# The end of a hybrid S5 and retention block: the first half's norm beside the last product, the last block taken from PSUM, rows of x loaded ahead, the last rows in halves

## The reference

```python
def reference(x, ...):                      # x: 1024 rows of 2048, float32
    h = rms_norm(x, norm_pre)
    proj = h @ w_in
    u_s, z_s, q, k, v, z_r, gl_s, gl_r = jnp.split(proj, SPLIT_IDX, axis=-1)
    y_s = s5_mixer(u_s, ...) * jax.nn.silu(z_s)
    y_r = retention(q, k, v) * jax.nn.silu(z_r)
    m = sigmoid(gl_s) * (y_s @ w_proj_s5) + sigmoid(gl_r) * (y_r @ w_proj_ret)
    return x + rms_norm(m @ w_out, norm_post)

def rms_norm(x, gain):
    return x * rsqrt(mean(x * x, axis=-1) + EPS) * gain
```

## Time and profile before

| What | Value |
|---|---|
| median of 3 runs | 2310.22 us (2309.75 to 2310.89) |
| profiled execution, time | 2312.22 us |
| profiled execution, span from first to last instruction | 2310.4 us |
| TensorE, share of the span | 96% |
| VectorE | 79% |
| ScalarE | 51% |
| mean rate of the DMA engines | 210 GB/s |
| mean granted TensorE clock | 0.99 |

### The profile page before, as it was taken

One profiled execution on the slowest core, in us unless ns is written; L12 is line 12 of the kernel. 1 busy time (PEld: TensorE's weight loads), 2 busy tenths in 40 slices (PEclk: granted clock), 3 DMA queues, 4 the chain that ended last, 5 costly groups with the idle time before them and its releaser, 6 DMA issues.

```text
span 2310.4 us, 28465 instructions
## 1 busy us (share of the span) xinstructions
PE 2212.9 (96%) x10212; PEld 1817.7 (79%) x10212; DVE 1814.9 (79%) x2937; ACT 1177.3 (51%) x1974; POOL 122.4 (5%) x200
## 2 busy tenths in 40 slices
PE   6989999999999999999989999999999999999993
PEld 3778788788888888888867878888888788788883
DVE  4986996888898888655897867766788889977676
ACT  4334444556665455564434645755545554445552
POOL 5240000000000000000000000200000000000000
PEclk9999999999999999999999999999999999999997
DMA  7347558776577365579755789575846755644546
GB/s 259 146 164 219 155 169 270 251 256 216 179 263 241 106 234 169 200 261 325 235 174 155 257 264 281 170 239 191 304 142 202 238 178 187 247 166 130 161 134 268
DMA packets 265854, 485.58 MB, mean 210 GB/s; under 512 B 51648, under 2 KB 59856, under 8 KB 263536
## 3 DMA queue, kind: packets, MB, share of 16 engines
q1 hardware_dynamic: 218336, 398.54, 52.4%
q10 hardware_dynamic: 37712, 50.47, 6.3%
q0 software_dynamic: 9664, 34.75, 4.7%
HBM read 367.28 MB, written 116.39 MB: 209 GB/s over the span
## 4 chain that ended last, share of the span: by engine, by line
PE 75%; DVE 14%; DMA 5%; issue 3%; ACT 2%; ACTq 0%; SPq 0%; DVEq 0%
PE psum L1803 18%; PE psum L1805 18%; PE psum L1804 18%; PE psum L1799 6%; PE psum L1801 6%; PE psum L1800 5%; DMA araw<-aops 4%; DVE a_lo L1291 3%; DVE b_lo L1293 3%; DVE work L1545 1%; ACT a_hi L886 1%; DVE keep L1301 1%; DVE work L1257 1%; PE psum L1740 1%; PE psum L1822 1%
## 5 line engine op out<-in xcount | busy, mean ns | idle before, releaser
L1803 PE MATMUL psum<-a_hi,b_hi 128*128 128x512 f32 x2352 | 923.5, 393 | 32.5 <-DVE b_lo L1293 32.1
L1805 PE MATMUL psum<-a_lo,b_hi 128*128 128x512 f32 x2352 | 918.1, 390 | 0.0
L1804 PE MATMUL psum<-a_hi,b_lo 128*128 128x512 f32 x2352 | 917.5, 390 | 0.0
L886 ACT ACTIVATE a_hi<-araw 128x512 fp32r<-128x512 f32 x644 | 406.0, 630 | 875.8 <-PE psum L1805 642.8
L1291 DVE TENSOR_TENSOR a_lo<-araw,a_hi 128x512 fp32r<-128x512 f32 x644 | 444.8, 691 | 348.4 <-ACT a_hi L886 345.3
L1803 PEld LDWEIGHTS psum<-a_hi,b_hi 128*128 128x128 f32 x2352 | 443.0, 188 | 138.1 <-DVE b_lo L1293 40.1
L1805 PEld LDWEIGHTS psum<-a_lo,b_hi 128*128 128x128 f32 x2352 | 442.9, 188 | 93.2
L1804 PEld LDWEIGHTS psum<-a_hi,b_lo 128*128 128x128 f32 x2352 | 443.4, 188 | 91.7 <-issue 0.7
L1293 DVE TENSOR_TENSOR b_lo<-bx,b_hi 128x512 fp32r<-128x512 f32 x432 | 296.8, 687 | 0.0
L895 ACT ACTIVATE b_hi<-bx 128x512 fp32r<-128x512 f32 x432 | 266.4, 617 | 1.6 <-DMA bx<-in_wstream 1.5
L1799 PE MATMUL psum<-b_hi,a_hi 128*128 128x512 f32 x672 | 263.1, 392 | 3.8 <-DVE b_lo L1293 3.4
(11 more groups left out here) (161 smaller groups left out, 1609.5 us busy)
## 6 DMA issues: line engine op xcount, KB each, us to landing
araw<-aops SPq DMA_DIRECT2D x632, 256.0 KB, 3.0
bz<-in_wstream SPq DMA_DIRECT2D x216, 256.0 KB, 4.5
aops<-work SPq DMA_DIRECT2D x28, 1024.0 KB, 6.8
spill<-keep ACTq DMA_DIRECT2D x28, 1024.0 KB, 6.1
bx<-in_wstream SPq DMA_DIRECT2D x108, 256.0 KB, 4.4
by<-in_wstream SPq DMA_DIRECT2D x108, 256.0 KB, 5.3
work<-spill SPq DMA_DIRECT2D x20, 1024.0 KB, 7.3
aops<-work POOLq DMA_DIRECT2D x15, 1024.0 KB, 7.1
```

The source lines that it names most:

```text
L886: A.activation(a_hi[:, r, :], left(s), ACT.Copy).then_inc(head, 1)
L1803: T.matmul(bank, b_hi[:, r, cols], a_hi[:, r, :], start=first, stop=False, skip_group_check=on)
L1804: T.matmul(bank, b_lo[:, r, cols], a_hi[:, r, :], start=False, stop=False, skip_group_check=on)
L1805: done = T.matmul(bank, b_hi[:, r, cols], a_lo[:, r, :], start=False, stop=last, skip_group_check=on)
```

## The change

- SP loads rows 2 to 7 of x during GO1, at steps 44, 46, 48, 50, 53 and 55: rows 2 and 3 into `by`, rows 4 and 5 into `bz`, rows 6 and 7 into `keep` blocks 3 and 2. The loads behind the last split are gone.
- VectorE makes the weights' differences for p = 6 of GO1 during p = 5, behind the splits of the same step, and no longer three steps ahead.
- ScalarE squares the block of p = 5 in two pairs, at steps 51 and 52, in place of four pieces at 52.
- The sum and root of the first half come at step 53, the reciprocal and row 0 at 54, row 1 at 55; rows 2 and 3 follow behind the last splits.
- The block of p = 6 is not evacuated: ScalarE squares its four pieces in PSUM, and VectorE multiplies each by the gain from PSUM once its square is done, the sum of squares before the last piece.
- Rows 4 to 7 are finished and stored in halves of 1024 columns, 512 KB each.

```diff
@@ -242,7 +242,10 @@
         o_row = area(0, 16384).rearrange("p (i n) -> p i n", i=8)
         gain_row = area(16384, 2048)
         x_ring = area(18432, 4096).rearrange("p (s n) -> p s n", s=2)
-        x_late = [by[:, 0:4, :], by[:, 4:8, :], bz[:, 0:4, :], bz[:, 4:8, :]]
+
+        x_rest = {n: b.rearrange("p k m -> p (k m)") for n, b in
+                  ((2, by[:, 0:4, :]), (3, by[:, 4:8, :]), (4, bz[:, 0:4, :]), (5, bz[:, 4:8, :]))}
+        x_rest[6], x_rest[7] = keep[:, 3, :], keep[:, 2, :]
 
         sq_ring = keep[:, :, :]
         rstd = araw[:, 0:2, :]
@@ -638,16 +641,31 @@
                     sp.wait_ge(op_stored[S4], 64)
                     for n in range(2):
                         sp.dma_start(x_ring[:, n, :], x[n]).then_inc(rows_loaded[n], 16)
-            sp.wait_ge(split, 2 * STEPS)
+                if g == GO1 and at in (44, 46):
+                    n = at // 2 - 20
+                    sp.wait_ge(split, 2 * (step_of(g, 4, TILES[g] - 1) + 1))
+                    sp.wait_ge(rows_loaded[n % 2], 16)
+                    sp.dma_start(x_rest[n], x[n]).then_inc(rows_loaded[n % 2], 16)
+                if g == GO1 and at in (48, 50):
+                    n = at // 2 - 18
+                    sp.wait_ge(gained, n - 2)
+                    sp.wait_ge(out_squared, 16 if n == 6 else 20)
+                    sp.wait_ge(rows_loaded[n % 2], 32)
+                    sp.dma_start(x_rest[n], x[n]).then_inc(rows_loaded[n % 2], 16)
+                if g == GO1 and at in (53, 55):
+                    n = (at - 45) // 2
+                    sp.wait_ge(split, 2 * (step_of(g, 5, TILES[g] - 1) + 1))
+                    sp.wait_ge(summed, sums_before(g, 6, TILES[g] - 1) + 1)
+                    sp.dma_start(x_rest[n], x[n]).then_inc(late_loaded, 16)
             for n in range(4):
-                sp.dma_start(x_late[n].rearrange("p k m -> p (k m)"), x[4 + n]).then_inc(late_loaded, 16)
-            for n in range(2, 4):
-                sp.wait_ge(rows_ready, n - 1)
-                sp.dma_start(x_ring[:, n % 2, :], x[n]).then_inc(rows_loaded[n % 2], 16)
-            for n in range(8):
                 sp.wait_ge(rows_ready, n + 1)
                 sp.dma_start(out[n], o_row[:, n, :]).then_inc(out_stored, 16)
-            sp.wait_ge(out_stored, 8 * 16)
+            for n in range(4, 8):
+                for half in range(2):
+                    sp.wait_ge(rows_ready, 2 * n - 3 + half)
+                    cols = slice(D_MODEL // 2 * half, D_MODEL // 2 * (half + 1))
+                    sp.dma_start(out[n][:, cols], o_row[:, n, cols]).then_inc(out_stored, 16)
+            sp.wait_ge(out_stored, 12 * 16)
 
 
         @block.gpsimd
@@ -980,18 +998,21 @@
                 else:
                     act.dma_start(spilled(g, b), kept_4(b)).then_inc(kept_stored[b], 16)
 
-            def squares(g, p):
+            def squares(g, p, first=0, blocks=4):
 
                 b = KEEP[p]
-                if p == 6:
+                if (g, p) == (GO1, 6):
+                    act.wait_ge(step_done, STEPS)
+                elif p == 6:
                     act.wait_ge(act_evac, 4 * g + 4)
                 else:
                     act.wait_ge(dve_evac, 3 * g + p - 2)
-                for n in range(4):
+                for n in range(first, first + blocks):
                     count = 16 * (g - GO0) + 4 * (p - 3) + n
                     if count:
                         act.wait_ge(out_squared, count)
-                    A.activation(m_junk, kept_4(b)[:, n, :], ACT.Square,
+                    block_n = main_banks(g)[:, n, :] if (g, p) == (GO1, 6) else kept_4(b)[:, n, :]
+                    A.activation(m_junk, block_n, ACT.Square,
                                  accum_out=ssq[:, 4 * HALF_OF[b] + n, 2 * (g - GO0) + COL_OF[b]:2 * (g - GO0) + COL_OF[b] + 1]
                                  ).then_inc(out_squared, 1)
 
@@ -1090,7 +1111,7 @@
                 if s == 2:
                     root(1)
                 over = ended(s - 3)
-                if over and over[1] in (0, 1, 2, 6):
+                if over and over[1] in (0, 1, 2, 6) and over != (GO1, 6):
                     evacuate(*over)
                 if over == (GV, 6):
                     take_m2()
@@ -1101,7 +1122,11 @@
                 if over == (GGR0, 6):
                     retain()
                 over = ended(s - 5)
-                if over and over[1] >= 3:
+                if ended(s - 4) == (GO1, 5) or ended(s - 5) == (GO1, 5):
+                    squares(GO1, 5, 2 * (s - BASE[GO1] - 51), 2)
+                elif ended(s - 1) == (GO1, 6):
+                    squares(GO1, 6)
+                elif over and over[1] >= 3 and over != (GO1, 6):
                     if over[0] in (GO0, GO1):
                         squares(*over)
                     else:
@@ -1119,7 +1144,7 @@
                 if s == BASE[GGS1] + 34:
                     shift(1)
                 for i in range(2):
-                    if s == STEPS + (2, 6)[i]:
+                    if s == (BASE[GO1] + 53, STEPS + 2)[i]:
                         act.wait_ge(out_sum, i + 1)
                         A.activation(rstd_out[:, 4 * i:4 * i + 4], rstd_out[:, 4 * i:4 * i + 4], ACT.Sqrt, scale=1.0 / D_MODEL,
                                      bias=eps_sb[:, 0:1]).then_inc(out_std, 1)
@@ -1555,7 +1580,9 @@
                 b = KEEP[p]
                 i = HALF_OF[b]
                 col = COLS * (2 * (g - GO0) + COL_OF[b])
-                if p == 6:
+                if (g, p) == (GO1, 6):
+                    dve.wait_ge(step_done, STEPS)
+                elif p == 6:
                     dve.wait_ge(act_evac, 4 * g + 4)
                 else:
                     dve.wait_ge(dve_evac, 3 * g + p - 2)
@@ -1563,6 +1590,14 @@
                     dve.wait_ge(gain_row_loaded, 16)
                     for op in (A11, S4, S3, A12, A22):
                         dve.wait_ge(op_stored[op], 64)
+                if (g, p) == (GO1, 6):
+                    for n in range(4):
+                        if n == 3:
+                            sum_rows(1)
+                        dve.wait_ge(out_squared, 28 + n + 1)
+                        V.tensor_tensor(o_row[:, 4 + n, col:col + COLS], main_banks(g)[:, n, :], gain_row[:, col:col + COLS],
+                                        ALU.mult).then_inc(gained, 1)
+                    return
                 V.tensor_tensor(o_row[:, 4 * i:4 * i + 4, col:col + COLS], kept_4(b),
                                 gain_row[:, col:col + COLS].unsqueeze(1).broadcast_to([P, 4, COLS]), ALU.mult).then_inc(gained, 1)
 
@@ -1576,15 +1611,17 @@
 
             def finish_row(n):
                 dve.wait_ge(out_inverse, n // 4 + 1)
-                dve.wait_ge(gained, 7 + n // 4)
-                if n < 4:
-                    dve.wait_ge(rows_loaded[n % 2], 16 * (n // 2 + 1))
-                    rows = x_ring[:, n % 2, :]
-                else:
-                    dve.wait_ge(late_loaded, 4 * 16)
-                    rows = x_late[n - 4].rearrange("p k m -> p (k m)")
-                V.scalar_tensor_tensor(o_row[:, n, :], o_row[:, n, :], rstd_out[:, n:n + 1], rows, ALU.mult, ALU.add
-                                       ).then_inc(rows_ready, 1)
+                dve.wait_ge(gained, 7 if n < 4 else 11)
+                if n in (4, 5):
+                    dve.wait_ge(late_loaded, 2 * 16)
+                else:
+                    dve.wait_ge(rows_loaded[n % 2], 16 * {0: 1, 1: 1, 2: 2, 3: 2, 6: 3, 7: 3}[n])
+                rows = x_ring[:, n, :] if n < 2 else x_rest[n]
+                parts = 1 if n < 4 else 2
+                for part in range(parts):
+                    cols = slice(D_MODEL // parts * part, D_MODEL // parts * (part + 1))
+                    V.scalar_tensor_tensor(o_row[:, n, cols], o_row[:, n, cols], rstd_out[:, n:n + 1], rows[:, cols], ALU.mult, ALU.add
+                                           ).then_inc(rows_ready, 1)
 
             for s in range(STEPS + TAIL):
                 if s < STEPS:
@@ -1596,7 +1633,7 @@
                 scanning = 0 <= c < CHUNKS
                 if scanning:
                     scan_products(c)
-                if s + RING < STEPS and not (TILES[place(s + RING)[0]] == 4 and place(s + RING)[1] == 6):
+                if s + RING < STEPS and not (place(s + RING)[1] == 6 and (TILES[place(s + RING)[0]] == 4 or place(s + RING)[0] == GO1)):
                     weights_summed(s + RING)
                 if s < STEPS and TILES[g] == 4 and p == 4:
                     weights_summed(step_of(g, 6, k))
@@ -1604,6 +1641,8 @@
                     scan_sum(c, 0)
                 if s < STEPS:
                     rests(s)
+                if s < STEPS and g == GO1 and p == 5:
+                    weights_summed(step_of(g, 6, k))
                 if scanning:
                     scan_sum(c, 1)
                 over = ended(s - 3)
@@ -1627,8 +1666,14 @@
                     gate_product(GATE_STEP[s])
```

(28 more changed lines are left out.)

## The result

The changed kernel takes **2291.91 us** in the median of 4 runs (2290.64 to 2293.36), the kernel before, beside it, 2310.01 us; the ratio is 0.9922, with a 95% interval of 0.9906 to 0.9938.

The account below looks back on a forecast made before the run. Tail without TensorE bounds it: VectorE's steps, a late x row, a transfer backlog. VectorE's rebuilt chain ends 2290.8, last store 2294.2, plus 0.45 closing: 2294.7, from the median 2294.5; range 2292.5 to 2298.5, the forecast case's own 2292.8 to 2296.

Parts of the forecast that it names:

- First half's norm: Steps 53 to 54: ScalarE's table load and root, 1.49 us together after the sum, start head 54 1.76 us late.
- What bounds the kernel: 35.1 us tail without TensorE, set by VectorE's ten large steps, a late x row and a transfer backlog.
- Loads ahead: Six x row loads during steps 44 to 55 cost 0 us, at most 0.4 per row; 6.71 us wait and backlog go.
- Differences moved, squares in pairs: Differences moved eight steps forward cost 0; third block's squares in two pairs start head 53 at 2261.95.
- Rows 0 and 1: VectorE at steps 54 and 55: row 0 ends 2270.5, splits of 55 at 2271.75, leaving TensorE 0.6 us spare.
- Last block in PSUM: 1.88 us evacuation goes; squares end 2278.4, products and reciprocal 2281.15, PSUM priced as SBUF, up to 0.4 more.
- Halves: Last rows as eight 1024-column steps, 1.20 us apart: 9.6 us against 9.04 for four full rows, VectorE ending 2290.8.
- Stores: No backlog left at the first half; the last 512 KB store lands in 3.2 us plus 0.2, at 2294.2.
- head 54 later: Rival, 0.18: load or a handover costs 1.0 to 2.5 us more, delaying VectorE's chain; 2295.5 to 2297.0 us.
- The stores set the end: Rival, 0.12: the last half store still takes 8.0 us to land; 2299.3, by the median 2299 us.
- The work eats the gain: Rival, 0.06: row steps before the splits make TensorE miss 2.72 us steps; two missed give 2299.9, four 2305.4.
- Slower: Rival, 0.02: x loads hold back araw, TensorE loses 5.9 us six times; 2329.9 us.

Follow-up runs that it names:

- e1: Changed kernel with a one-column ScalarE copy that waits for the first half's sum, so the table load comes behind the sum; 2292.62 us, ratio 0.9928.
- e2: Changed kernel with a one-column root at step 20 of the last group, so the table load is done long before the end; 2289.51 us, ratio 0.9913.
- first experiment: Kernel before and changed kernel rerun unaltered, kernel before also with one ScalarE copy added; medians 2310.13 and 2309.79, 2290.93, and 2307.10 us.
- e3: Kernel before with only the x rows loaded during the last group and the weights' differences moved forward; 2303.39 us, ratio 0.9974.
- e5: Changed kernel with the last block evacuated to SBUF by ScalarE as before, squared and multiplied there; 2291.29 us, ratio 0.9919.
- e6: Changed kernel with rows 4 to 7 finished and stored whole instead of in halves; 2291.34 us, ratio 0.9919.
- e4: Changed kernel with the first half's norm, and rows 0 to 3, only behind the product; 2300.26 us, ratio 0.9957.
- e7: Changed kernel with all six x row loads issued at once at step 52; 2301.84 us in its one run.
- a0: Changed kernel run once more, unaltered; 2290.93 us in the median of 6 runs.
- e8: Changed kernel with row 3 finished on GpSimd instead of VectorE; 2299.17 us, ratio 0.9964.

## Why the prediction was wrong, step by step

The chain was right, one term of it was off by 1.3 us, and the end of the product, which the forecast left where it was, moved as well. Against the start of the last matmul (2274.89 in the forecast, 2273.19 in the profile after):

| Point | forecast | measured |
|---|---|---|
| head 54 starts | -8.6 | -10.0 |
| row 0 starts | -6.7 | -8.0 |
| splits of step 55 done | -3.1 | -4.4 |
| first product from PSUM | +3.6 | +2.3 |
| first half row starts | +6.3 | +5.0 |
| VectorE done | +15.9 | +14.6 |
| end of the span | +19.8 | +18.4 |

Every line is off by the same 1.3 to 1.4 us, and the first one already is. **The failed step is "First half's norm", where it says "ScalarE then needs table load 1.28 and root, 1.49 together before the next": the load was put behind the sum.** It ran ahead of the wait for the sum, right behind head 53, and was hidden. e1 forced it behind, and the tail rose by 1.5 us (1.28 and the 0.2 of the copy); e2 removed it, and nothing changed. The term measured 0.20 us (2262.96 to 2263.16) instead of 1.49. The text had named this way out, inside its own range only and at 0.8 us, for which it gives no working; e1 gives 1.3 (the rise less the copy's 0.2). Its lower bound, 2292.8, doesn't follow from its terms either: 2294.5 less 0.8 and 0.6 is 2293.1.

The term alone doesn't take the time out of the range. The tail's gain of 17.1 us on the first median gives 2293.1 (2310.22 - 17.1), inside it; 2291.9 lies 1.2 us lower. The forecast kept the last matmul at 2274.9, put nothing for all that lies ahead of it, and named a move of over 1 us as a sign that it is wrong. It moved by 1.7, and that sign came true. The reason for putting nothing was a spread of 0.05%, taken from three runs; 21 runs of the kernel before spread from 2304.7 to 2314.1, 0.4%. So the 1.2 us are less than executions of one program differ by, and whether they are chance or an effect of the edit stays open (first experiment).

The other steps, in their order. *What bounds the kernel*: it counts ten large steps of VectorE in the tail, the rows show nine (eight row steps and the product). *Loads ahead*: right, no stop of TensorE and araw landing in 4.8 us at most; 4.9 us of the gain by e3. *Differences moved, squares in pairs*: TensorE lost nothing, and head 53 starts 13.1 us ahead of the last matmul against 12.9 forecast. *Rows 0 and 1*: right in length; the cover at step 55 was 1.9 us (splits done 4.4 ahead of the last matmul's start, the step's first matmul 2.5 ahead) and not 0.6, and even e1, with 0.4, kept TensorE going. *Last block in PSUM*: squares at 0.72 us against 0.75 forecast, products at 0.60; worth 1.2 us by e5. *Halves*: 2278.16 to 2287.82 are 9.66 us against 9.6 forecast; worth 0.75 us by e6. *Stores*: end 3.8 us behind VectorE against 3.9.

Undone one at a time, the parts give 4.9 (e3 on the kernel before), 9.1 (e4), 1.2 (e5) and 0.75 (e6), 15.9 of the 17.1 us. The 1.2 us left may be the parts' effect on one another (undone singly, each finds the others in place); no run shows it.

Of the rivals, *head 54 later* is refuted: no handover cost more than forecast. In e1 the load starts 0.01 us behind the copy and the root 0.02 behind the end of the load (2259.43 + 1.28 = 2260.71, 2260.73). The drain of 1.38 us that the Trainium skill (ScalarE: Activation LUTs, What ACT_TABLE_LOAD costs) counts at each switch doesn't show there. *The stores set the end* is refuted: the last half lands in 3.3 us. *The work eats the gain*: TensorE has no gap. *Slower*: not here, but e7 shows its mechanism at 6.9 us.

## What to carry to other kernels

Before costing a root or an exponential at a hand-over, look whether a table load can start before the semaphore it precedes: an idle ScalarE hides it, and it costs where it lies behind the wait (e1, e4). A tail of row steps and stores can be rebuilt as one engine's chain from start-to-start distances; here each piece behind the norm came out within 0.1 us. And a small change of a long kernel is measured from a late landmark of the trace, not from the median: here the tail repeats to 0.1 to 0.3 us where the time spreads over 9.

## What the runs showed of the hardware

A table load need not be held by the wait of the instruction it serves: in the changed kernel it started 1.5 us before the sum that its root waited for, and so it did in a0, e5, e6 and e8. In e7, where head 53 was late, it started only 0.7 us before the sum (2270.12 against 2270.82), and the root came 0.01 us behind the load, 0.4 us behind the sum: hidden in part. Where ScalarE waited for two semaphores (e4) it stayed behind them. Whether their number decides, or which engine sets them, was not tried.

GpSimd and VectorE hold each other up: in e8 VectorE's split grew from 0.68 to 4.14 us and its row step from 2.35 to 6.60, while the row step between them kept its length (2.34). The long row step ends 2.1 us behind the end of GpSimd's second instruction, about its own length alone, as if it had waited for that one to finish. The Trainium skill (SBUF — State Buffer, SBUF: two separate sides) says that a port pair shared by the two is taken for a whole instruction, and that the other engine blocks. The trace agrees for GpSimd's second instruction; its first is recorded until 2270.75, 1.3 us into a row step of VectorE at full speed, and GpSimd's spans are rough.

After the stop of 5.4 us in e7 TensorE's matmuls started 0.43 us apart instead of 0.227, eight times in a row (2270.96 to 2274.39), and then 0.23 again. The granted clock of 2272 to 2276 us, which holds both, is 0.68, a mixture of the 1.2 and 2.4 GHz levels. After e8's stop of 1.8 us (2267.79 to 2269.62) the clock of 2270 to 2272 us is 1.00. The window of 2272 to 2276 us of e7, the clock in the third column from the right:

```profile
2272.00:2276.00 4.00, 4.00 (x14) 3.19 (x13) 3.71 (x5) 1.79 (x4) 0.00 (x0) 0.68 0.00 0
```
